# State-space scan on one core: fp32r spreads of split sums, heads in alternating pairs, samples on column and row groups of TensorE

## The reference

```python
acum = jnp.cumsum(dtc * A, axis=2)
xd = xc * dtc[..., None]
seg = at[..., :, None] - at[..., None, :]
decay_ls = jnp.exp(jnp.where(causal, seg, -jnp.inf))
cb = jnp.einsum('bclgn,bcsgn->bcgls', Cc, Bc)
y_diag = jnp.einsum('bcgrls,bcsgrp->bclgrp', cb[:, :, :, None] * decay_ls, xd)
states = jnp.einsum('bclgn,bclgrp->bcgrpn', Bc, xd * decay_end[..., None])
y_off = jnp.einsum('bclgn,bcgrpn->bclgrp', Cc, prev) * jnp.exp(acum)[..., None]
```

## Time and profile before

| | us |
|---|---|
| median of 3 runs | 3422.87 (3421.79 to 3426.29) |
| the profiled execution, its own time | 3424.1 |
| its span, first to last instruction | 3422.4 |
| PE busy | 3194.8 |
| DVE busy | 1475.7 |
| ACT busy | 1150.5 |
| POOL busy | 273.1 |

### The profile page before, as it was taken

How to read it: one execution, slowest core, us unless ns; L and a number is a source line. 1 busy time by engine, 2 the same in 40 slices (tenths; PEclk the granted TensorE clock), 3 DMA queues, 4 the chain that set the end, 5 groups by cost and what they waited for, 6 DMA issues and landing times.

```text
span 3422.4 us, 55224 instructions
## 1 busy us (share of the span) xinstructions
PE 3194.8 (93%) x22296; PEld 2932.4 (86%) x22296; DVE 1475.7 (43%) x2112; ACT 1150.5 (34%) x1631; POOL 273.1 (8%) x364
## 2 busy tenths in 40 slices
PE   6999998999999979989999899999897889899996
PEld 5899997888887856989999789999895567899996
DVE  4444426776767232254442534442431052544423
ACT  3433323444444223233332323332212142333322
POOL 0000000222222010000000000000001101000000
PEclk9999999999999989999999999999998898999998
DMA  6422322322232224222232242232322602223231
GB/s 200 132 86 86 89 85 59 100 74 76 84 90 71 94 74 135 86 62 86 86 89 85 59 143 86 86 89 84 103 83 67 216 10 62 63 86 88 84 91 51
DMA packets 444958, 306.48 MB, mean 90 GB/s; under 512 B 12516, under 2 KB 415644, under 8 KB 444700
## 3 DMA queue, kind: packets, MB, share of 16 engines
q1 hardware_dynamic: 421780, 231.03, 23.2%
q0 software_dynamic: 19744, 69.48, 6.0%
q10 hardware_dynamic: 3328, 4.47, 0.4%
HBM read 282.73 MB, written 22.20 MB: 89 GB/s over the span
## 4 chain that ended last, share of the span: by engine, by line
PE 89%; DVE 6%; ACT 2%; issue 1%; DMA 1%; ACTq 0%; POOL 0%; SPq 0%; DVEq 0%; POOLq 0%
PE PS L967 58%; PE PS L1210 8%; PE PS L1036 5%; PE PS L1013 2%; PE PS L1158 2%; PE PS L1170 1%; PE PS L1131 1%; PE PS L1109 1%; DVE yT L1516 1%; DVE rb L1501 1%; PE PS L1268 1%; PE PS L1247 1%; PE PS L1341 1%; PE PS L1148 1%; PE PS L1280 1%
## 5 line engine op out<-in xcount | busy, mean ns | idle before, releaser
L1497 DVE TENSOR_TENSOR wlo<-raw,whi 128x1024 fp32r<-128x1024 f32 (+2 forms) x401 | 488.7, 1219 | 786.5 <-ACT whi L545 776.5
L967 PE MATMUL PS<-hH,whi 128*128 128x272 f32 x3280 | 682.7, 289 | 15.5 <-DVE hL L1512 7.6
L967 PE MATMUL PS<-hH,wlo 128*128 128x272 f32 x3280 | 681.1, 289 | 0.0
L967 PE MATMUL PS<-hL,whi 128*128 128x272 f32 x3280 | 678.5, 288 | 0.0
L545 ACT ACTIVATE whi<-raw 128x1024 fp32r<-128x1024 f32 (+2 forms) x401 | 412.9, 1030 | 618.6 <-PE PS L967 553.6
L967 PEld LDWEIGHTS PS<-hH,whi 128*128 128x128 f32 x3280 | 518.9, 189 | 18.3 <-issue 16.7
L967 PEld LDWEIGHTS PS<-hL,whi 128*128 128x128 f32 x3280 | 517.9, 189 | 0.0
L967 PEld LDWEIGHTS PS<-hH,wlo 128*128 128x128 f32 x3280 | 514.2, 190 | 0.0
L967 PE MATMUL PS<-H,whi 128*128 128x272 f32 x1984 | 411.4, 289 | 5.7 <-DVE L L1938 2.5
L967 PE MATMUL PS<-H,wlo 128*128 128x272 f32 x1984 | 411.9, 289 | 0.0
L967 PE MATMUL PS<-L,whi 128*128 128x272 f32 x1984 | 410.3, 288 | 0.0
(11 more groups left out here) (362 smaller groups left out, 3763.4 us busy)
## 6 DMA issues: line engine op xcount, KB each, us to landing
raw<-in_w_ffn_gu SPq DMA_DIRECT2D x176, 512.0 KB, 3.7
kvr<-in_cache_mem_kv POOLq DMA_DIRECT2D x32, 1024.0 KB, 5.9
raw<-in_w_in_a SPq DMA_DIRECT2D x57, 512.0 KB, 3.7
raw<-in_w_ffn_down SPq DMA_DIRECT2D x64, 448.0 KB, 3.6
rawm<-in_w_mem_kv SPq DMA_DIRECT2D x32, 512.0 KB, 4.5
raw<-in_w_ffn_down SPq DMA_DIRECT2D x32, 512.0 KB, 4.0
raw<-in_w_out_a SPq DMA_DIRECT2D x24, 512.0 KB, 3.7
raw<-in_w_in_b SPq DMA_DIRECT2D x20, 512.0 KB, 3.6
```

The source lines that it names most:

```text
L967: mm = pe.matmul(PS[:, bank + h, 0:HT], w[:, slot, k * P:(k + 1) * P], x[:, h * HT:(h + 1) * HT], start=first and w is whi and x is hi_k, ...
L1497: dve.tensor_tensor(wlo[:, slot, 0:nk * P], src, whi[:, slot, 0:nk * P].bitcast(F32), ALU.subtract).then_inc(s["w_lo"], 1)
```

## The change

1. The spreads become fp32r products. `acHL` has 64 rows: the sums rounded to fp32r, and below them the rest. `selg` picks the same row in both halves. VectorE makes `acHL` once, and copies one more column block per group.
2. Heads are multiplied in pairs, `heads(p)`, alternately one product of the even and one of the odd head.
3. The samples' token-major tiles stand four times, once in each block of 32 partitions. GpSimd makes four copies side by side before the transposes (`xs4`), which then wait for it (`cz_ready`) and move behind the prompt's transposes. The off-diagonal products of samples 0 to 3, and then 4 to 7, go to four blocks of 32 output partitions; a later addition picks from the transposed result what belongs together. The new states' products take their 32 rows from another block each. `BZ` has 4 blocks of 128 columns on 128 partitions instead of 8 on 32.
4. Order. TensorE: `spread(1)` moves ahead of the state transposes and the second tile; heads 0 and 1 stand where head 0 stood, heads 2 and 3 where head 3 stood. VectorE: both differences of a pair come before its two masks, and the low part and the convolution behind them. ScalarE: `pair_decay(1)` and `pair_decay(3)` move ahead of the copies of the next group's tiles.

```diff
@@ -330,17 +330,20 @@
...
-        selg = A1("selg", [NH, 4])
+        selg = A1("selg", [2 * NH, 4], F32R)
+        acHL = A1("acHL", [2 * NH, T], F32R)
...
-        EAS = A1("EAS", [NS, NH])
+        EAS = A1("EAS", [P, NH])
...
-        EASg = A1("EASg", [NS, 4])
+        EASg = A1("EASg", [P, 4])
...
-        tmpL = A1("tmpL", [NH, NS])
+        smp4 = A1("smp4", [NH, 3, P])
+        xs4 = A1("xs4", [P, 3, P])
+        four_t = lambda ap: ap.unsqueeze(1).to_broadcast([ap.shape[0], 4, NS])
...
@@ -845,14 +848,14 @@
...
                         decay(1)
+                        pair_decay(1)
                         ahead(1)
-                        pair_decay(1)
                         decay(2)
...
                         state_rows(1)
+                        pair_decay(3)
                         ahead(2)
-                        pair_decay(3)
                         act.wait_ge(s["final_ready"], gx(g, 1, 1))
...
@@ -1244,7 +1248,7 @@
...
-                            pe.matmul(PS[:, 2, :], selg[:, h:h + 1].to_broadcast([NH, P]), acum[:, 0:SEQ], start=True, stop=True).then_inc(s["bc_ready"], 1)
+                            pe.matmul(PS[:, 2, :], selg[:, h:h + 1].to_broadcast([2 * NH, P]), acHL[:, 0:SEQ], start=True, stop=True).then_inc(s["bc_ready"], 1)
...
@@ -1256,19 +1260,22 @@
...
-                        def head(h):
-
-                            pe.wait_ge(s["m_ready"], gx(g, 4, h + 1))
-                            pe.wait_ge(s["c_ready"], gx(g, 4, h + 1))
-                            if h == 0:
+                        def heads(p):
+
+
+                            pe.wait_ge(s["m_ready"], gx(g, 4, 2 * p + 2))
+                            pe.wait_ge(s["c_ready"], gx(g, 4, 2 * p + 2))
+                            if p == 0:
...
-                            r, w = (h % 2) * PD, slice(h * PD, (h + 1) * PD)
+                            pair = [(h * PD, slice((2 * p + h) * PD, (2 * p + h + 1) * PD), h) for h in range(2)]
...
-                                pe.matmul(PS[r:r + PD, 6 + h // 2, c * P:(c + 1) * P], xd[:, c, w], Lh[:, h % 2, c * P:(c + 1) * P], start=True, stop=c == 0)
-                                if c:
-                                    pe.matmul(PS[r:r + PD, 6 + h // 2, c * P:(c + 1) * P], ST[:, c - 1, w], Eh[:, h % 2, c * P:(c + 1) * P], start=False, stop=True)
-                            pe.matmul(PS[r:r + PD, 3, 128 + (h // 2) * NS:128 + (h // 2 + 1) * NS], xd[0:NS, NCH, w], Lh[0:NS, h % 2, SEQ:T], start=True, stop=True).then_inc(s["y_used"], 1)
+                                for r, w, h in pair:
+                                    pe.matmul(PS[r:r + PD, 6 + p, c * P:(c + 1) * P], xd[:, c, w], Lh[:, h, c * P:(c + 1) * P], start=True, stop=c == 0)
+                                for r, w, h in pair if c else ():
+                                    pe.matmul(PS[r:r + PD, 6 + p, c * P:(c + 1) * P], ST[:, c - 1, w], Eh[:, h, c * P:(c + 1) * P], start=False, stop=True)
+                            for r, w, h in pair:
+                                pe.matmul(PS[r:r + PD, 3, 128 + p * NS:128 + (p + 1) * NS], xd[0:NS, NCH, w], Lh[0:NS, h, SEQ:T], start=True, stop=True).then_inc(s["y_used"], 1)
...
@@ -1277,7 +1284,8 @@
...
-                                mm = pe.matmul(PS[:, 4 + k, :], xdd[0:NS, NCH, q * P:(q + 1) * P], BZ[:, 4 * k:4 * k + 4, :].rearrange("p b n -> p (b n)"), start=True, stop=True)
+                                r = slice((2 * q + k) * NS, (2 * q + k + 1) * NS)
+                                mm = pe.matmul(PS[:, 4 + k, :], xdd[r, NCH, q * P:(q + 1) * P], BZ[r, :, :].rearrange("p b n -> p (b n)"), start=True, stop=True)
...
@@ -1289,17 +1297,18 @@
...
-                        for q, t in enumerate((0, 2, 3)):
-                            pe.transpose(PS[0:NS, 3, q * P:(q + 1) * P], xt(t)[:, SEQ:T], ident)
-                        pe.matmul(PS[0:NS, 3, 384:384 + NS], xt(0)[:, SEQ:T], xt(1)[:, SEQ:T], start=True, stop=True)
-                        for q in range(2):
-                            pe.matmul(PS[:, 3, 416 + q * NB:416 + (q + 1) * NB], selp[:, 2 * q:2 * q + 2, :].rearrange("p a b -> p (a b)"), acum[:, SEQ + NT - 1:T:NT], start=True, stop=True)
...
-                            tr = pe.transpose(PS[:, 2, c * P:(c + 1) * P], xt(0)[:, c * P:(c + 1) * P], ident)
-                        tr.then_inc(s["tok_ready"], 1)
+                            pe.transpose(PS[:, 2, c * P:(c + 1) * P], xt(0)[:, c * P:(c + 1) * P], ident)
+                        pe.wait_ge(s["cz_ready"], gx(g, 1, 1))
+                        for q in range(3):
+                            pe.transpose(PS[:, 3, q * P:(q + 1) * P], xs4[:, q, :], ident)
+                        pe.matmul(PS[0:NS, 3, 384:384 + NS], xt(0)[:, SEQ:T], xt(1)[:, SEQ:T], start=True, stop=True)
+                        for q in range(2):
+                            mm = pe.matmul(PS[:, 3, 416 + q * NB:416 + (q + 1) * NB], selp[:, 2 * q:2 * q + 2, :].rearrange("p a b -> p (a b)"), acum[:, SEQ + NT - 1:T:NT], start=True, stop=True)
+                        mm.then_inc(s["tok_ready"], 1)
...
@@ -1312,7 +1321,7 @@
...
-                            mm = pe.matmul(PS[:, 3, h * NS:(h + 1) * NS], selg[:, h:h + 1].to_broadcast([NH, P]), acum[:, SEQ:T], start=True, stop=True)
+                            mm = pe.matmul(PS[:, 3, h * NS:(h + 1) * NS], selg[:, h:h + 1].to_broadcast([2 * NH, P]), acHL[:, SEQ:T], start=True, stop=True)
...
@@ -1322,14 +1331,13 @@
...
                         mm.then_inc(s["st_ready"], 1)
+                        spread(1)
                         state_rows(0)
                         ahead(1, 0)
-                        spread(1)
                         ahead(1, 1)
-                        head(0)
+                        heads(0)
                         spread(2)
                         ahead(2, 0)
-                        head(1)
                         spread(3)
...
@@ -1338,18 +1346,18 @@
...
                         for b in range(NB):
-                            mm = pe.matmul(PS[0:NS, 2, 0:256], CZ[:, b, :], S0T[:, b, :], start=b == 0, stop=b == NB - 1)
+                            r = b % 4 * NS
+                            mm = pe.matmul(PS[r:r + NS, 2, 0:256], CZ[:, b, :], S0T[:, b, :], start=b < 4, stop=b >= 4)
                         mm.then_inc(s["yoff_ready"], 1)
                         new_states(0)
-                        head(2)
                         ahead(3, 0)
-                        head(3)
+                        heads(1)
                         pe.wait_ge(s["yos_ready"], gx(g, 1, 1))
...
                         for q in range(2):
-                            tr = pe.transpose(PS[:, 3, 192 + q * NS:192 + (q + 1) * NS], yos[:, q * P:(q + 1) * P], ident[0:NS, 0:NS])
+                            tr = pe.transpose(PS[:, 3, 192 + q * P:192 + (q + 1) * P], yos[:, q * P:(q + 1) * P], ident)
                         tr.then_inc(s["y_ready"], 1)
...
@@ -1761,20 +1769,23 @@
...
-                    dve.tensor_copy(tmpL[:, :].rearrange("p (b t) -> p b t", b=NB), acum[:, SEQ + NT - 1:T:NT].unsqueeze(2).to_broadcast([NH, NB, NT])).then_inc(s["scan_done"], 1)
+                    dve.tensor_copy(smp4[:, 0, :].rearrange("p (f t) -> p f t", f=4), four_t(acum[:, SEQ:T]))
+                    dve.tensor_copy(smp4[:, 1, :].rearrange("p (f t) -> p f t", f=4), four_t(dtx[:, SEQ:T]))
+                    st(dve.tensor_copy(smp4[:, 2, 0:NS].rearrange("p (b t) -> p b t", b=NB), acum[:, SEQ + NT - 1:T:NT].unsqueeze(2).to_broadcast([NH, NB, NT])))
+                    st.wait()
+                    dve.tensor_copy(smp4[:, 2, NS:].rearrange("p (f t) -> p f t", f=3), smp4[:, 2, 0:NS].unsqueeze(1).to_broadcast([NH, 3, NS])).then_inc(s["scan_done"], 1)
+                    st(dve.tensor_copy(acHL[0:NH, :], acum[:, :]))
+                    st.wait()
+                    st(dve.tensor_tensor(acHL[NH:2 * NH, :], acum[:, :], acHL[0:NH, :].bitcast(F32), ALU.subtract))
...
-                    for t in (aT, dT, CD):
-                        st(dve.memset(t[:, NCH, :], 0.0))
...
-                    for m, c0, c1 in ((P, 0, NCH), (NS, NCH, NCH + 1)):
-                        w = slice(c0 * NH, c1 * NH)
-                        for q, dst in enumerate((aT, dT, CD)):
-                            st(dve.tensor_copy(dst[0:m, c0:c1, :].rearrange("p c h -> p (c h)"), PS[0:m, 6, q * 160 + w.start:q * 160 + w.stop]))
+                    for q, dst in enumerate((aT, dT, CD)):
+                        st(dve.tensor_copy(dst[:, :, :].rearrange("p c h -> p (c h)"), PS[:, 6, q * 160:(q + 1) * 160]))
...
@@ -1794,7 +1805,8 @@
...
-                        dve.tensor_copy(selg[:, :], con[0:NH, hs])
+                        dve.tensor_copy(selg[0:NH, :], con[0:NH, hs])
+                        dve.tensor_copy(selg[NH:2 * NH, :], con[NH:2 * NH, bass.ds(gx(g, 4, NH), 4)])
...
@@ -1866,27 +1877,25 @@
...
                         chunk_states()
+                        seg(1)
+                        masked(0)
```

(29 more changed lines are left out.)

38 lines of the change are left out of this document (19 added, 19 removed).

## The result

The changed kernel takes **3372.07 us** (median of 4 runs, 3371.1 to 3375.93) against 3422.33 us (3421.07 to 3426.29) for the kernel before in the same session: ratio 0.9853, 95% interval 0.9836 to 0.987. It is 50 us faster, where 57 were forecast (3366 us, range 3352 to 3408). The profiled executions differ by 53.0 us in their spans, 3422.4 and 3369.4 us.

A forecast was written before the change was run, and what follows sets the result against it. TensorE, busy 93% of the span, was taken as the bound. Savings of 8.95 us per group less 0.5 of waits gave 59 us in seven groups; less 1.2 at the start, net 58: 3366 us, range 3352 to 3408.

The forecast's parts named there:

- likeliest case: Whole kernel: the author's own forecast, 3352 to 3376 us, chance 0.47.
- Part 1: Decay spreads as fp32r products: large ones 1.05 to 0.30 us, 3.0 us saved per group; small ones 0.3 saved.
- Part 2: Heads multiplied in alternating pairs: full overlap brings a pair from 3.82 to 2.15-2.2 us, saving 3.2 us per group.
- Part 3: Samples' products on several column and row groups: off-diagonal term saves 1.55 us per group, new states 0.85.
- in-order rule: TensorE starts its records in order; the off-diagonal products on four column groups then need nine steps, 2.0 us.
- Part 4: Added work per group: wider sample-output transposes lose 0.15 us, fewer projection-to-head entries gain 0.2, GpSimd copies stay hidden.
- Part 5: New order: TensorE waits for VectorE's masks and low part, 0.5 us per group for both places, ends 0 and 2.
- rival 2: VectorE becomes the bound: 2 us of waits per group gives 3377 us, 4 gives 3391; within a shared chance of 0.23.
- mark of a wrong forecast: Sign set beforehand: TensorE waiting over 10 us in all for other engines in the seven groups.
- Rival 1: Heads and samples: column groups do not overlap, only 22 us saved, 3402 us; chance 0.19 (3396 to 3412).
- Rival 3: Heads and off-diagonal term: each change of column group waits, 3.2 us lost per group, 3447 us; chance 0.08.
- Rival 4: Spreads: fp32r does not run one column per step, no gain there, 3389 us; within a shared chance of 0.23.

The follow-up runs named there:

- Both spread experiments: The kernel before with only the fp32r spreads added, 3398.18 us; and the changed kernel with fp32 spreads put back, 3390.06 us.
- e_yord: Changed kernel with the samples' off-diagonal products reordered so that products for one column group are neighbours; 3361.07 us in one run, 3369.26 us when timed again.
- e_fp32spread: Changed kernel with the fp32r spreads put back to fp32, all else as changed; 3390.06 us, ratio 0.9911.
- e_seq: Changed kernel with all products of a pair's first head before those of the second; 3375.37 us, ratio 0.9872.
- b_nst2: Kernel before, with the second half of the samples' new states in a buffer of its own; 3416.37 us, ratio 0.9978.
- e_both: Changed kernel with the new states' second half in buffer S0T and the split sums acHL made after tile 3's low part; 3354.95 us, ratio 0.9801.

## Why the prediction was right, and where it was not

The time is 6 us from the forecast and inside the likeliest case's own range (3352 to 3376). That it came so close is in part luck. The pieces saved 76 us in seven groups where 8.95 x 7 = 63 were forecast, and waits and clock took back 20 where 3.5 were forecast: two errors that took each other away.

**Part 1, spreads: right, low by little.** 0.30 was taken for a spread, with 0.45 as the bad end; it is 0.43, so 0.62 is saved and not 0.75. The small ones took 0.35 instead of 0.5. Together 2.9 per group against 3.3. Both spread experiments gave 3.4 per group; the rest is waits and clock, as reckoned there.

**Part 2, heads: the overlap was right, its count low.** 2.15 to 2.2 us per pair was the forecast with records in strict order; it is 1.91, the same as one head: 3.8 us saved per group instead of 3.2. A product still takes two steps in its own column group (0.22 us for 128 columns), as forecast; that one step more was needed at the end, and 0.35 for the sample products, was not (0.23).

**Part 3, samples: the strict order failed.** That "by the same in-order rule, nine steps remain: 2.0 us" was wrong. 16 records took 1.00 us, as long as four and a half steps of 0.223, so four column groups run abreast; 2.57 us saved, the end of the range that I had put at 2.6. e_yord shows the same from another side: with neighbours in one column group the block takes 1.02. The new states saved 0.85 + 0.67 = 1.5 instead of 0.85: the two row groups overlap nearly wholly.

**Part 4, added: one cost missed, one not there.** The first block of state transposes takes 1.04 us where it took 0.87, since `spread(1)` now stands right in front of it. The second block stood behind a spread before as well and took 1.02. In e_fp32spread, where the spread is fp32, the first block takes 1.02 too: it isn't the number format. Both kinds of spread use fewer than 128 rows of the array (32 and 64), the transposes all 128. This costs 0.17 us per group. The wider `yos` transposes cost nothing instead of 0.15: their two records take 0.22 us in e_seq where they took 0.24. The two entries that go from projections to heads gave the 0.2 forecast: the eight halves of a group take 24.9 us in e_seq and 25.1 before. TensorE waited for GpSimd in no group.

Sum of these pieces: 2.5 + 0.46 + 3.8 + 2.57 + 1.5 - 0.17 + 0.02 + 0.2 = 10.9 us per group against the 8.95 forecast, 76 us in seven.

**Part 5, the order: one place right, one mis-sized.** The masks were just in time: in group 2 the second mask's large operation ran from 757.91 to 758.58, heads(0) started at 758.73 behind a projection product, and no row has TensorE waiting for a mask in groups 0 to 6; 0 to 0.5 us had been put there. At the low part behind the new states I had called VectorE and TensorE level and put 0.5 us per group on it, ends 0 and 2. TensorE waited 10.4 + 3.7 + 0.7 = 14.8 us in the seven groups for other engines, 2.1 per group. This is the size of **rival 2**, and over the 10 us that I had named as the mark of a wrong forecast. The step that failed is the balance at that place. I let VectorE begin the new states where the off-diagonal products end, as it did before (0.6 us behind them). With the change those products come sooner while VectorE's work ahead of the new states does not, and it began 4.8 us behind them. In group 1 VectorE's low part then ended at 730.78, 19.5 us behind the off-diagonal products, where 18.0 had been reckoned at most; TensorE was through with all before it at 729.13, after 17.8 us instead of 18.3. I had listed the DMA in VectorE's chain as a part that stays. Its wait grew little, from 14.3 to 17.1 us in seven groups; what changed is that the 17.7 us in which VectorE waited for TensorE's new states right behind it are gone, so that nothing hides it any more:

```profile
L1872 DVE TENSOR_TENSOR nst<-S,cds 128x1024 f32<-128x1024 f32 x14 | 17.1, 1221 | 17.1 <-DMA out_ssm_s<-nst 17.1
```

That row is of the changed kernel's groups of instructions, 619 to 1035 us (busy, mean ns of one, idle before and its releaser). Rival 2 was named rightly, but VectorE was not full: it was late by the order of its work and held by a transfer. This window of group 1 has it busy for 46.6 of 58.5 us (PE, PEld, DVE, ACT, POOL):

```profile
680.00:738.50 58.50, 56.12 (x448) 50.86 (x447) 46.55 (x100) 29.62 (x58) 15.52 (x26) 0.97 0.36 95
```

**Where 76 became 56.6.** All of TensorE's waits in the stretch, issue included, are 20.5 us instead of 7.7: 12.8 lost. The clock's loss is 10.4 us instead of 3.5: 6.9 more, by the estimate above; no run takes the clock alone. 76.2 - 12.8 - 6.9 = 56.5, for the measured 56.6. The forecast had no term for the clock.

**The ends.** Group 7: forecast 0 give or take 3, measured 1.1 lost. The start: 1.2 us forecast, 2.6 measured between two profiled executions, of which not all is the change's. VectorE's timeline of the changed kernel there:

```profile
594.06 0.21 DVE L1772 COPY smp<-acum 32x128 f32<-32x128 f32 x1
...
594.70 0.42 DVE L1777 CAST acHL<-acum 32x544 fp32r<-32x544 f32 x1
595.16 0.72 DVE L1779 TENSOR_TENSOR acHL<-acum,acHL 32x544 fp32r<-32x544 f32 x1
595.90 1.22 DVE L1505 TENSOR_TENSOR wlo<-raw,whi 128x1024 fp32r<-128x1024 f32 x1
```

The low part ends at 597.12 instead of 594.24, 2.9 later. Of this 1.1 stood there already at the low part before the last one (584.37 against 583.23), ahead of all that was added, so the added work is 1.7, and 0.7 of slack was there: 1.0 lost, close to the forecast. TensorE then ran eight halves in 26.02 us against 24.46; the window from 590 to 623 us has a granted clock of 0.95 where it was 1.00. This isn't the change's: b_nst2, whose start is that of the kernel before, took 25.98 us for them and began group 0 at 624.5 us, and e_both, which has the change, took 24.47. So the start can't be judged to better than some 4 us from one execution of each kernel.

**The range.** Its low end took 0.9 for the new states and 1 us of waits, although their own best ends were 1.8 and 0. The new states saved 1.5, beyond what the range allowed for.

**The rivals.** Rival 1 (no overlap) fell with e_seq: 1.90 us for one head, 1.91 for two. Rival 3 (alternation serialises, slower) fell with the same rows. The Trainium skill ("TensorE: Matmul & The Clock Gate", section "Part 3: Packing small matmuls") says that weight loads overlap running products only when the row group differs. Here both heads use all 128 rows and alternate, and nothing is lost to their loads, so the measurement decides against reading that rule as a price for column groups. The same section's 2.38x for three column tiles is 0.79 per tile; here it is 3.57 / 1.00 = 3.57x for four, 0.89 per tile. Rival 4 (the fp32r spread at a lower rate) fell with 0.43 us.

## What to carry to other kernels

When a step takes work from the busiest engine, look for waits of the second engine that lie just behind what the first one delivers: they cost nothing as long as the first one is late, and become the bound once it is early. Here a single buffer between VectorE and an outgoing DMA was worth 0 us before the change, 3.5 with the heads one after the other and 13 with all of the change. Measure such an edit by a mark that recurs in the trace from the first to the last group: one and the same kernel gave 411.5 and 410.5 us there, while the same two executions took 3361.07 and 3372.76 us. Count the waits over that same stretch in each kernel; a window fixed in microseconds cuts off the end of the slower one.

## What was not expected of the hardware

- Two-record fp32 products for different column groups overlap completely, with the same rows of the array: two heads in 1.91 us, one in 1.90; four groups of 256-column products in 1.00 us instead of 3.57. Two row groups of 512-column products into two banks: 1.06 us instead of 1.91.
- The order of the products among the column groups doesn't matter (1.00 and 1.02 us): in these two orders a record that waits for its column group did not hold back the others.
- Eight 128-row transposes take 0.87 us behind a 128-row product and 1.02 to 1.04 behind a spread of 32 or 64 rows, whether this is fp32 or fp32r.
- The granted clock fell from 0.96 to 0.50 behind a single wait of 3.1 us, and e_seq, with 26.6 us more work and fewer waits, ran its stretch at a mean of 0.992 against 0.975: work taken away at the cost of waits bought less than its length.
